# Moving six of every eight down-weight loads from the SP queue to the ACT queue

## The reference

```python
gates = route(x)                       # 64 experts, 8 chosen per token
hid = silu(x @ w_gate[e]) * (x @ w_up[e])        # w_gate, w_up: 1024 x 256
y = sum over e of (hid * gates[:, e]) @ w_down[e]   # w_down: 256 x 1024
y = y + (silu(x @ ws_gate) * (x @ ws_up)) @ ws_down
```

## Time and profile before

| | us |
|---|---|
| median of 3 runs | 1734.3 (1732.55 to 1734.37) |
| the profiled execution's own time | 1731.31 |
| span of the profiled execution | 1729.5 |
| PE busy in the span | 1629.2 (94%) |
| DVE, ACT, POOL busy | 419.8, 282.5, 80.3 |
| HBM read | 507.64 MB, 294 GB/s over the span |
| first experts' pair starts, layer 0 and layer 1 | 404.5 and 1258.1 |

### The profile page before, as it was taken

One profiled execution on the slowest core, in us unless ns is written; L12 is line 12 of the kernel. 1 busy time (PEld: TensorE's weight loads), 2 busy tenths in 40 slices (PEclk: granted clock), 3 DMA queues, 4 the chain that ended last, 5 costly groups with the idle time before them and its releaser, 6 DMA issues.

```text
span 1729.5 us, 20756 instructions
## 1 busy us (share of the span) xinstructions
PE 1629.2 (94%) x7908; PEld 903.8 (52%) x7909; DVE 419.8 (24%) x858; ACT 282.5 (16%) x550; POOL 80.3 (5%) x124
## 2 busy tenths in 40 slices
PE   6999999989999999989889999999899999999996
PEld 5878668564333334333367885775633333333332
DVE  2141211043222222222222302111422222222223
ACT  1032002121111111111120410110211111111111
POOL 2000002030000000000010000200400000000000
PEclk9999999999999999999989999999999999999998
DMA  9165343448999999999870744425499999999995
GB/s 298 64 252 182 126 148 151 146 146 317 420 418 421 418 422 422 419 422 422 318 287 1 292 146 170 146 104 189 154 375 414 421 421 418 422 422 419 422 422 210
DMA packets 115603, 509.65 MB, mean 295 GB/s; under 512 B 12768, under 2 KB 16960, under 8 KB 73040
## 3 DMA queue, kind: packets, MB, share of 16 engines
q1 hardware_dynamic: 110592, 508.59, 74.0%
q10 hardware_dynamic: 4720, 0.02, 0.3%
q0 software_dynamic: 224, 0.12, 0.1%
HBM read 507.64 MB, written 1.05 MB: 294 GB/s over the span
## 4 chain that ended last, share of the span: by engine, by line
PE 79%; DMA 10%; SPq 5%; DVE 2%; issue 2%; ACT 1%; DVEq 0%; ACTq 0%; POOL 0%; POOLq 0%
PE work L685 38%; PE work L990 20%; PE work L1021 9%; DMA ring<-in_w_up 9%; SPq L509 5%; PE moe_sum L944 3%; PE work L901 3%; PE moe_sum L889 1%; PE work L711 1%; PE work L1008 1%; PE moe_sum L936 1%; PE work L908 0%; ACT hidden L1204 0%; PE work L779 0%; DMA par_all<-in_w_conv 0%
## 5 line engine op out<-in xcount | busy, mean ns | idle before, releaser
L990 PE MATMUL work<-ring,arena 128*64 128x512 f32 x1216 | 287.0, 596 | 21.0 <-DMA ring<-in_w_up 14.7
L685 PE MATMUL work<-XT,ring 128*128 128x256 f32 x1280 | 279.4, 380 | 1.1 <-DVE arena L1441 1.1
L685 PEld LDWEIGHTS work<-XT,ring 128*128 128x128 f32 x1280 | 243.7, 191 | 36.0 <-DVE arena L1441 1.9
L990 PEld LDWEIGHTS work<-ring,arena 128*64 128x64 f32 x1216 | 90.1, 137 | 168.2 <-issue 156.1
L1021 PE MATMUL work<-ring,hidden 128*64 128x512 f32 x768 | 175.4, 598 | 1.0 <-DVE hidden L1635 1.0
L685 PE MATMUL work<-ring,arena 128*128 128x512 f32 (+1 forms) x336 | 140.6, 579 | 8.3 <-DVE arena L1484 3.4
L1642 DVE TENSOR_TENSOR out_lo<-work,out_hi 128x512 fp32r<-128x512 f32 x128 | 88.6, 692 | 231.1 <-ACT out_hi L1229 231.1
L1631 DVE SCALAR_TENSOR_TENSOR hidden<-hidden,slot_gate,work 128x256 f32<-128x256 f32 x64 | 30.7, 480 | 418.5 <-ACT hidden L1225 418.5
L1229 ACT CAST out_hi<-work 128x512 fp32r<-128x512 f32 x128 | 75.1, 587 | 213.6 <-PE work L1021 213.6
L685 PEld LDWEIGHTS work<-ring,arena 128*128 128x128 f32 x336 | 63.3, 190 | 82.7 <-issue 72.9
L1225 ACT ACTIVATE hidden<-work 128x256 f32<-128x256 f32 x64 | 24.6, 385 | 492.3 <-PE work L990 492.3
(11 more groups left out here) (218 smaller groups left out, 1455.1 us busy)
## 6 DMA issues: line engine op xcount, KB each, us to landing
ring<-in_w_gate SPq DMA_DIRECT2D x96, 1024.0 KB, 17.8
ring<-in_w_up SPq DMA_DIRECT2D x96, 1024.0 KB, 20.6
ring<-in_w_down SPq DMA_DIRECT2D x96, 1024.0 KB, 17.0
arena<-in_w_gate SPq DMA_DIRECT2D x32, 1024.0 KB, 20.3
arena<-in_w_up SPq DMA_DIRECT2D x32, 1024.0 KB, 21.5
arena<-in_w_down SPq DMA_DIRECT2D x32, 1024.0 KB, 17.9
ring<-in_w_in SPq DMA_DIRECT2D x28, 1024.0 KB, 13.0
ring<-in_w_mix_out SPq DMA_DIRECT2D x8, 1024.0 KB, 12.7
```

The costliest lines, as they stand in the source:

```text
L685: mm = pe.matmul(dst, a, b, start=(k == 0), stop=(k == len(pairs) - 1))
L990: mm = pe.matmul(work[0][rows, :], xg[b][c][:, k * P + e * TT * SLOTS:k * P + (e + 1) * TT * SLOTS], w, start=(c == 0), stop=(c == KC - 1))
```

## The change

Six of the eight down loads of a body, those of q = 2 to 7, are no longer issued by SP. ACT issues the down load of pair q + 2 right behind the SiLU of pair q, for q = 0 to 5, with no wait of its own: it has already waited for the gate and up matmuls of pair q, which free the buffer. The down loads of q = 0 and 1 of every body stay with SP, at their place in its order. SP skips the others, with their waits.

```diff
                     for m in units:
+                        if m % 3 == 2 and m >= 8:
+                            continue
                         wait_unit_read(m, pairs, halves, first)
                         load_unit(m, pair_firsts[m // 3], first)
 
+            e_down = w_down.rearrange("l e (p k) d -> (l e) p k d", k=2)
+
+            def load_down(q, expert):
+
+                u = (3 * q + 2) % UNITS
+                for i in range(2):
+                    act.dma_start(unit[u][:, i * SLOT // 2:(i + 1) * SLOT // 2].rearrange("p (k n) -> p k n", k=2),
+                                  e_down[bass.ds(expert + i, 1)].rearrange("o p k d -> (o p) k d")
+                                  ).then_inc(slot_loaded[u], 16)
+
                         halves = act.snap((base + r * BODIES + i) * (2 * BODY_PAIRS))
+                        experts = act.snap(l * EXPERTS + i * (2 * BODY_PAIRS))
                         batch = act.snap((base + r * BODIES + i) * 2 + l)
                             act.activation(hid, work[0][:, 0:EXPERT_DIM], ACT.Silu).then_inc(silu_ready, 1)
+                            if q + 2 < BODY_PAIRS:
+                                load_down(q + 2, act.snap(experts + 2 * (q + 2)))
                             take_gather(1 - b, 2 * k, 3, (batch + (b + 1)) * (KC // 2) + (k + 1))
```

## The result

The changed kernel takes 1753.63 us (median of four runs, 1752.06 to 1754.17), the one before 1733.70 on the same chip (four runs, 1732.55 to 1734.37): ratio 1.0114, 95% interval 1.0097 to 1.0132. That is 19.9 us slower where 23 were forecast; the time lies inside the range. The profiled execution took 1752.06 us with a span of 1750.2, 20.7 more than the span of before.

What follows compares the result with a forecast made beforehand. The full DMA stream bounds the kernel; pair 30's load landing sets each layer's end. Later start 3.5 plus overtaking 8.0 is 11.5 us per layer, 23 for both, giving 1757 us from 1734.3; range 1748 to 1764.

Steps and rivals of the forecast that it cites:

- What bounds it: In the expert plateaus PE follows the full DMA stream; a layer ends a fixed rest after pair 30's load lands.
- Part 1: SP drops six loads per body; its next loads go out earlier only by the issue time, gain 0.
- Part 2: At a layer's start ACT issues pair 2's down load later than SP did, so the stream starts 3.5 us later.
- Part 3: Down loads on ACT's queue overtake SP's; pair 30's load lands 8.5 us later, 7.6 followed pair by pair, 8.0 taken.
- pair 29 starts 14.9 us before L: L is the landing of pair 30's load; 6.4 us shared at half rate put 3.2 us of down 31 ahead.
- upper bound of 10.3: Largest overtaking delay of pair 30's load, in us, if ACT's loads go ahead of all of SP's.
- the sum: Later start plus overtaking, 3.5 + 8.0 = 11.5 us per layer, 23 us for both layers, nothing hidden between them.
- The clock: In layer 0's plateau TensorE's granted clock is 1.00, its upper level, and was said to play no part.
- Part 4: ACT's two DMA issues between SiLU and the gather copy take about 1 us, within 3.8 us of cover: cost 0.
- A: Rival: loads are served in order of issue, without overtaking; only the later start costs, 7 us, 1741; chance 0.10.
- B: Rival: two queues raise the plateau's rate; at 3% it takes off 26.6 us, giving 1730.7; chance 0.07.
- C: Rival: ACT's two issues take 8.3 us, delaying the copy in the two later bodies: 53 us, 1810; chance 0.08.

Runs made afterwards that it cites:

- experiment 2: Changed kernel, but ACT issues only the down loads of q = 6 and 7 of each body: 1757.52 us against 1732.64 for the kernel before, ratio 1.0133.
- Experiment 3: Changed kernel, but ACT issues only the down loads of q = 2 and 3 of each body: 1750.69 us against 1732.64 for the kernel before, ratio 1.0100.
- 4: Kernel before, SP alone; in looped bodies a pair's down load goes ahead of its second gate and up load: 1744.20 us against 1732.64, ratio 1.0065.
- experiment 1: Kernel before, but pair 2's down load in each layer waits for all of pair 0's gate and up matmuls: 1736.28 us against 1732.64, ratio 1.0019.
- experiment 9: Kernel before, but pair 2's down load in each layer waits for the end of pair 0's down matmuls: 1745.45 us against 1732.06, ratio 1.0087.
- experiment 6: Kernel before, with every pair's gate and up weights cut into halves, in 4 KB packets: 1743.43 us against 1732.89, ratio 1.0060.
- experiment 8: Changed kernel, with gate and up of q = 2 and 6 also cut into halves: 1755.72 us against 1732.89 for the kernel before, ratio 1.0133.

## Why the prediction was right, and where it was off

**What bounds it: right.** Every experiment that puts another load ahead of the one that PE waits for makes the kernel slower by about that load (2, 3, 4), a hole in the stream costs half to three quarters of itself by the medians (1, 9), and a lower rate costs too (6).

**Part 1, 0 us: not tested by itself.** The plateau after is as high as the one before, so there is no room in it for a gain.

**Part 2, 3.5 us per layer: right for the stream, too large as a cost by itself.** ACT's issue falls at 411.65, and the stream ramps up from 412.6, as it did from 409.3 before:

```profile
412.60:413.60 1.00, 0.48 (x4) 0.28 (x5) 0.42 (x1) 0.59 (x1) 0.00 (x0) 1.00 0.41 131
416.00:832.00 416.00, 397.44 (x2132) 154.61 (x2130) 97.65 (x171) 64.71 (x120) 0.00 (x0) 0.98 1.01 421
```

The last byte of layer 0 lands at 855.6 (pair 31's second gate and up load, issued at 829.45, 26.1 us) where it was 852.5: 3.1 us later. The stream had no other hole. But experiment 1, which has this hole and nothing else, took 3.6 us more by the medians (interval 1.7 to 4.9) and 5.5 in the experts of its trace, where twice the hole of 3.1 to 3.5 would be 6.2 to 7; experiment 9 took 13.4 for twice 9.2. What takes up the rest stays open.

**Part 3, the overtaking: the mechanism right, the size at pair 30 too large.** How the queues share is plain in the packets of each (the queue lines from 764 to 769 us, in which a down load and a gate or up load are both under way; columns as in the earlier trace rows):

```profile
q10 hardware_dynamic: 146, 1.07, 51.1%
q1 hardware_dynamic: 145, 1.06, 50.8%
```

One packet for one, half the rate for each, now for large loads, as foretold. The turn goes by packets and not by bytes: from 840 to 844 us, where SP's load is in halves and so in packets of 4 KB, ACT's queue has 142 packets and SP's 153, but 1.07 MB and 0.60.

The page "DMA: Bandwidth & Descriptors" of the Trainium skill, section "Queues, rings and completion order", says that an engine takes packets in turn from the rings that it has work for; this trace agrees.

But of the 8.0 us that pair 30's load should lose by this, it lost 5.0: it landed 840.4 - 832.3 = 8.1 us later, 3.1 of which are part 2. Its row in the trace (issue time; then, to landing, us):

```profile
L509 SPq DMA_DIRECT2D ring<-in_w_up x1: 383/383/383, 815.9 to 815.9; - x1
DMA to landing us min/median/max: 24.5/24.5/24.5
```

Two assumptions of the working failed.

First, "packets begin 1 us later", taken from the idle engines of a layer's start. In a full stream ACT's first packets move about 3.5 us after the issue. The down load of pair 26 goes out at 758.35; the queue lines of 760.35 to 761.85 and then of 761.85 to 763.85 read

```profile
q1 hardware_dynamic: 84, 0.63, 101.0%
...
q10 hardware_dynamic: 59, 0.48, 57.8%
q1 hardware_dynamic: 55, 0.38, 45.4%
```

and at the down loads of pairs 14, 20, 27, 30 and 31 it was the same, with at most two packets in the half microsecond before. That takes 2.5 us of sharing away, 1.25 of the term.

Second, "pair 29 starts 14.9 us before L". It started at 829.34 and the load landed at 840.40, 11.1 us, since PE had been held back at pair 26 and was behind the stream. ACT issues at SiLU, so a PE that is late issues the overtaking loads late. That is 3.8 us less of sharing, 1.9 of the term. 8.5 - 1.25 - 1.9 = 5.3, against 5.0 in the trace. The issue of pair 31's down load shows both at once:

```profile
836.61 0.85 ACTq L1104 DMA_DIRECT2D arena<-in_w_down  x2
```

From 838 to 840 us only SP's queue moves packets (199 of them, none on q10), and 840.40 is the landing of pair 30's load. So down 31 takes next to nothing from it, and the 5.0 us are the one load down 30. That a late PE alone makes this difference was not isolated; experiment 8, in which PE is earlier and the loads behind come later, speaks for it but has the packets in it too. Of the 7.6 us that the prediction got by following the last body pair by pair it shows no working, so it can't be said why that missed pair 26.

**What set the end instead: pair 26.** Pair 26 is q = 2. Its own down load is the first of its body that ACT issues, while those of pairs 24 and 25 still stand in SP's order ahead of it. So between the second loads of pairs 25 and 26, which landed 14.9 us apart before (three loads of 5.0 us), now five land, down 25, down 26, down 27, and pair 26's own two: pair 25's, issued at 736.85, landed 24.0 us later, at 760.9, and pair 26's at 785.7, 24.8 us apart. The rows of its two up transfers, after and then before (issue times; then, to landing, us), give the difference:

```profile
L509 SPq DMA_DIRECT2D arena<-in_w_up x2: 382/728/1075, 745.2 to 751.0; - x2
DMA to landing us min/median/max: 30.5/32.6/34.6
```

```profile
L509 SPq DMA_DIRECT2D arena<-in_w_up x2: 2082/2088/2093, 741.3 to 745.7; - x2
DMA to landing us min/median/max: 26.3/26.6/26.9
```

751.0 + 34.6 = 785.7 against 745.7 + 26.9 = 772.6: 13.1 us later, 3.1 of part 2 and two down loads, 9.9. That is close to the term's upper bound of 10.3, which pair 26 meets almost in full. The prediction had the place wrong: it followed the last body and took pair 30 for the wait that comes last. From pair 26 PE has its own pace, which is faster than the stream, and gains back 73.9 - 71.3 = 2.6 us until pair 31; 13.1 - 2.6 = 10.4 us per layer, where 11.5 were forecast. So it is luck in part that the total came close: the 8.0 us stood at pair 30, whose load PE did not wait for at all, and pair 26, which the sum didn't have, cost about as much. Experiment 3 shows pair 26 by itself, experiment 2 pair 30 by itself, each about as dear as the whole. The two do not add: in the changed kernel pair 30's load lost 5.0 us to the passing loads, in experiment 2, where PE is on time, over 10.

**The clock plays a part after all.** It falls in the long wait. Two stretches, the end of the wait and the start of pair 26 (granted clock third from last):

```profile
778.00:785.80 7.80, 0.11 (x2) 0.03 (x1) 1.29 (x2) 0.06 (x1) 0.00 (x0) 0.64 1.02 423
785.80:788.00 2.20, 2.20 (x6) 0.82 (x8) 0.00 (x0) 0.00 (x0) 0.00 (x0) 0.50 1.00 417
```

After 7.7 us of idling, pair 26 begins at 0.50, the lower level of 1.2 GHz, and its 32 matmuls take 9.36 us instead of 7.09. Without these 2.3 us PE would have gained back up to 4.9 (an estimate: at its new time pair 30 would have met its load just as it landed). The length of a wait alone doesn't tell what follows: after 1.88 us of idling ahead of pair 21 the stretch from 708 to 711.5 us had a granted clock of 0.57, whereas in the kernel before the clock stayed at 1.00 after a wait of 2.48 us (743 to 745 us). What parts the two stays open.

**Part 4, ACT's own time: right.** The issues of down loads into the ring on ACT (those into the arena took 367 ns at most), and the copy behind one of them:

```profile
L1104 ACTq DMA_DIRECT2D ring<-in_w_down x64: 339/361/395, 411.6 to 1688.0; - x64
```

```profile
758.35 0.86 ACTq L1104 DMA_DIRECT2D ring<-in_w_down  x2
759.44 0.59 ACT L1212 COPY arena<-work 128x512 f32<-128x512 f32 x1 [0.95 <-PE work L903]
```

None took over 0.40 us, two in a row took 0.86, and the copy still comes after 0.95 us of idling, as the 0.96 of the earlier trace rows. PE never waits for the copy.

**The rivals.** A (no overtaking, 1741) is ruled out by the latencies and the packets, B (a faster stream, 1731) by the plateau of 421 GB/s, C (ACT held, 1810) by the ACT issues. C meets its hardest case in experiment 2, whose timeline has two of ACT's issues inside one of SP's that lasts 15 us:

```profile
699.62 15.15 SPq L509 DMA_DIRECT2D arena<-in_w_up  x1
...
708.39 0.85 ACTq L1104 DMA_DIRECT2D arena<-in_w_down  x2
```

**The sum.** 10.4 + 1.0 + 9.3 = 20.7 in the trace against 2 x 11.5 = 23. The upper end of the prediction's own range, 15 us per layer, is 1 more than its parts, 10.3 + 3.7 = 14.0; nothing measured lies near it. Most of the signs came true: PE's waits start at pair 14 (5.09 us), pair 30 starts at 842.9 (near 844 foretold), layer 1's experts at 1269.5 (near 1270). Pair 30's start fits for a wrong reason, PE's pace from pair 26 on and not the landing of its load. No version in the study beats the kernel before.

## What to carry to other kernels

Where a saturated stream of loads is the bound, ask in which order the loads land. Here a second queue took packets one for one, so a load put on it passed what waited in the first, and the loads wanted next paid for it; a second queue should get what is wanted next, not what can wait (no run here tried that). Look for the place in the loop where most passing loads fall between two that are waited for, here the first pair past the ones left in the old order, and follow the consumer from there: here it was held back early, so it issued later, and lost less behind. The load that starts the stream should stay with the engine that can issue it first.

## What the runs showed of the hardware that was not expected

- A DMA issued from ACT into a full stream moved its first packets about 3.5 us after the issue, in all six cases read in the changed kernel.
- Two queues took turns by the packet and not by the byte: against packets of 4 KB on SP's queue, ACT's packets of 8 KB got 1.07 MB while SP's got 0.60.
- With gate and up loads in packets of 4 KB (experiment 6) the stream ran at 412 GB/s, with 8 KB at 418 to 421, with the DMA share above 1 in both.
- A wait of PE of 3.5 us (experiment 8), 7.7 us (changed kernel) or 8.1 us (experiment 2) was followed by a stretch at the lower clock: the first 16 matmuls then took 5.35, 5.92 and 5.44 us, not 3.65. In the kernel before, with waits up to 2.5 us, the clock of the plateau was 1.00; in the changed kernel one wait of 1.9 us was followed by a granted clock of 0.57.
- One of SP's issues of 1 MB took 15 us (experiment 2), and ACT's two in the middle of it 0.85 us together: what held SP did not hold ACT.
